# Rope in the head, gate columns turned, decays masked first: a change to a two-layer hybrid encoder on one Trainium2 core

## What is computed

```python
h = rms_norm(x, norm_mix_g)
u = h @ w_in                       # four mixers' columns
o_na = neighbourhood_attention(...)
h_fwd = mlstm_scan(qm, km, vm, gates[0], log_sigmoid(gates[1]))
h_bwd = flip(mlstm_scan(flip(qm), flip(km), flip(vm), flip(gates[2]), flip(log_sigmoid(gates[3]))))
o_ml = rms_norm(h_fwd + h_bwd, ml_norm_g) * sigmoid(qkvo[:, :, 3])
o_cv = conformer_conv(u_cv, ...)
qd = axial_rope(rms_norm(qd, att_q_norm_g)); kd = axial_rope(rms_norm(kd, att_k_norm_g))
o_at = blocked_gqa(qd, kd, vd)
proj = einsum('bsnc,ncd->bsnd', branches, w_branch)
g = sigmoid(h @ w_gate + b_gate)
x = x + (sum(g * proj) @ w_out)
x = x + hierarchical_moe(rms_norm(x, norm_ffn_g), ...)
```

## Time and profile before

| what | value |
|---|---|
| median of three runs | 2245.08 us (2244.16 to 2246.12) |
| the profiled execution's own time | 2239.99 us |
| its span | 2238.2 us |
| TensorE matmul busy | 91% of the span |
| VectorE, ScalarE, POOL busy | 43%, 23%, 15% |
| mean granted TensorE clock | 0.962 of full speed |

### The profile page before, as it was taken

One profiled execution on the slowest core, in us unless ns is written; L12 is line 12 of the kernel. 1 busy time (PEld: TensorE's weight loads), 2 busy tenths in 40 slices (PEclk: granted clock), 3 DMA queues, 4 the chain that ended last, 5 costly groups with the idle time before them and its releaser, 6 DMA issues. The chain is left out here.

```text
span 2238.2 us, 24086 instructions
## 1 busy us (share of the span) xinstructions
PE 2045.4 (91%) x8840; PEld 1274.6 (57%) x8840; DVE 965.6 (43%) x1820; ACT 524.9 (23%) x1114; POOL 339.3 (15%) x276
## 2 busy tenths in 40 slices
PE   7799999999999997999498999999999999969990
PEld 3455556555655554888245555645555655558870
DVE  1677615343545644111256773243444475431114
ACT  2133312344330001111122332124353100101111
POOL 1322220111110011000223122102211100110003
PEclk9999999999999998999799999999999999979995
DMA  5355557111116622998441121212110274159955
GB/s 203 151 198 210 232 196 299 54 66 66 66 57 249 239 92 106 368 365 308 177 182 38 66 80 52 76 38 97 73 66 26 108 284 195 57 230 343 371 203 178
DMA packets 67188, 361.85 MB, mean 162 GB/s; under 512 B 5760, under 2 KB 6144, under 8 KB 54016
## 3 DMA queue, kind: packets, MB, share of 16 engines
q1 hardware_dynamic: 42160, 276.40, 32.8%
q10 hardware_dynamic: 18000, 58.73, 6.5%
q0 software_dynamic: 6912, 25.17, 3.1%
HBM read 249.13 MB, written 111.15 MB: 161 GB/s over the span
## 5 line engine op out<-in xcount | busy, mean ns | idle before, releaser
L674 PE MATMUL bank<-x,ring 128*128 128x384 f32 x1056 | 374.6, 504 | 27.1 <-issue 27.1
L674 PE MATMUL bank<-hT,ring 128*128 128x384 f32 x1056 | 360.2, 490 | 3.2 <-issue 3.2
L674 PEld LDWEIGHTS bank<-x,ring 128*128 128x128 f32 x1056 | 199.7, 195 | 187.5 <-issue 73.8
L674 PEld LDWEIGHTS bank<-hT,ring 128*128 128x128 f32 x1056 | 195.9, 190 | 144.9 <-issue 21.4
L832 ACT ACTIVATE sums<-bank 128x384 f32<-128x384 f32 x132 | 64.9, 491 | 306.1 <-PE bank L674 304.4
L994 DVE SCALAR_TENSOR_TENSOR reg_a<-cvx,pp,reg_a 128x783 f32<-128x783 f32 x120 | 130.3, 1086 | 4.3
L659 PE MATMUL bank<-ring,hT 128*128 128x256 f32 (+1 forms) x384 | 125.4, 486 | 0.0
L972 DVE SCALAR_TENSOR_TENSOR gbuf<-bank,sums 128x384 f32<-128x384 f32 x96 | 53.5, 558 | 155.3 <-PE bank L674 108.4
L1719 DVE SCALAR_TENSOR_TENSOR prob<-prob,bank 128x256 f32<-128x256 f32 x30 | 12.6, 421 | 229.4 <-ACT prob L1539 229.4
L659 PEld LDWEIGHTS bank<-ring,hT 128*128 128x128 f32 x384 | 72.5, 190 | 49.1 <-issue 43.7
L506 PE MATMUL bank<-ring,hT 128*128 128x512 f32 x192 | 88.2, 614 | 5.3 <-ACT hT L525 5.3
(11 more groups left out here) (258 smaller groups left out, 2991.1 us busy)
## 6 DMA issues: line engine op xcount, KB each, us to landing
ring<-in_wd SPq DMA_DIRECT2D x29, 2048.0 KB, 9.8
blocks<-hT SPq DMA_DIRECT2D x16, 3072.0 KB, 21.3
gate_dram<-gbuf ACTq DMA_DIRECT2D x64, 384.0 KB, 2.3
ring<-gate_dram SPq DMA_DIRECT2D x16, 1536.0 KB, 6.4
oT<-in_we SPq DMA_DIRECT2D x8, 2048.0 KB, 11.4
ring<-in_we SPq DMA_DIRECT2D x8, 2048.0 KB, 11.9
wide<-in_we SPq DMA_DIRECT2D x8, 2048.0 KB, 11.1
reg_b<-in_we SPq DMA_DIRECT2D x8, 2048.0 KB, 11.4
```

The source lines that it names most:

```text
L674: mm = nc.tensor.matmul(bank[i % 2][:, 0:HALF], w[:, k, :], a[:, k, :], start=(k == 0 and r in (0, 1, 3)), stop=(k == 3), skip_group_check ...
```

## The change

1. Layer 0's first chunk of weights is loaded in two halves, with tile 1 between them, and the projection of a tile waits for the second half only at its fifth k-step. In both layers ScalarE evicts tile 0's transposes ahead of tile 1's squares. In layer 1 POOL's power of tile 0 stands ahead of one of the gathers.
2. Rope 0 leaves the list. VectorE does its piece 0 in the head ahead of tile 5's variance, and pieces 1 and 2 after tile 5's scaling; POOL's power of 18 columns stands ahead of tile 5's power. The halves of the gate bias move with it.
3. The 16 gate columns are appended to the output gate's 256 (`GATE_ROWS`). ScalarE copies them into `gate_cols`, tiles of 128 columns that POOL sets to zero once, and in place of each `mg` unit TensorE transposes three of these tiles. ScalarE's step `ctanh` comes after the fourth unit of `mo`, not the fifth.
4. The weighing is a step of its own, `weigh`. Where a decay follows the scores, its mask comes first on VectorE and the weighing behind it. For a short group both `dexp` steps stand ahead of the product, and three products instead of two follow each of its score steps that has a decay; in the long groups the third and fourth score steps are followed by one product instead of two. The number of products is the same.

```diff
-        if u == T // 2 - 1:
-            for piece in range(3):
-                add("rope", 0, piece)
...
-        if u == 4:
+        if u == 3:
             add("ctanh")
...
-    def decay(n, *key):
+    def decay(n, *key, weigh=None):
         add("decay", *key)
+        if weigh:
+            add("weigh", *weigh)
         add("dexp", *key, 0)
-        gate(n)
-        add("dexp", *key, 1)
+        if GROUPS[key[0]][1] == 2:
+            add("dexp", *key, 1)
+            gate(n)
+        else:
+            gate(n)
+            add("dexp", *key, 1)
...
             if q + 1 < len(pairs) and j < 2:
-                decay(1, *pairs[q + 1], j)
-                gate(1)
+                decay(1, *pairs[q + 1], j, weigh=(g, hp, j))
+                gate(2 if GROUPS[g][1] == 2 else 1)
             else:
-                gate(2)
+                add("weigh", g, hp, j)
+                gate(1 if j >= 2 else 2)
...
-                sp.dma_start(ring[:, 0, :], wd[0]).then_inc(head_in[0], 16)
-                for t in range(1, T):
+                sp.dma_start(ring[:, 0, 0:CW // 2], wd[0][:, 0:CW // 2]).then_inc(first_half, 16)
+                sp.dma_start(x[:, 1, :], tile_of(1)).then_inc(x_in[1], 16)
+                sp.dma_start(ring[:, 0, CW // 2:CW], wd[0][:, CW // 2:CW]).then_inc(head_in[0], 16)
+                for t in range(2, T):
...
-            if layer == 0:
-                head_square(act, layer, 1)
-                evict(0)
-            else:
-                evict(0)
-                head_square(act, layer, 1)
+            evict(0)
+            head_square(act, layer, 1)
...
+            rope(dve, done, 0, 0)
+            variance(T - 1)
+            scale(T - 1)
+            rope(dve, done, 0, 1)
+            rope(dve, done, 0, 2)
...
+                rope_power(pool, 0)
+                power(T - 1)
                 return
-            for t in (2, 3):
-                for c in range(TOP):
-                    gather(pool, t, c)
+            gather(pool, 2, 0)
+            gather(pool, 2, 1)
+            gather(pool, 3, 0)
             power(0)
+            gather(pool, 3, 1)
...
+            def gate_rows(i, name, u):
+                pe.wait_ge(proj_ev[i % 2], i // 2)
+                evicted(pe, at[("proj", "mo", T // 2 * (u + 1) - 1)])
+                for t in range(T // 2):
+                    mm = nc.tensor.transpose(bank[i % 2][:, t * P:(t + 1) * P], gate_cols[:, T // 2 * u + t, :], ident)
+                mm.then_inc(proj_mm, 1)
...
+                    done(activate(mlo[:, u, :], b[:, 0:BW], ACT.Tanh, scale=0.5))
+                    ins = activate(gate_cols[:, u, :].rearrange("p (q r) -> p q r", q=4)[:, :, 0:HEADS],
+                                   b[:, BW:BW + GATE_ROWS].rearrange("p (q r) -> p q r", q=4), ACT.Copy)
```

More of the change, by code:

```diff
@@ L35 @@
 BW = 256
+GATE_ROWS = 16
 HEADS = 4
@@ L497, in head_tensor @@
                     if k == 0:
-                        pe.wait_ge(head_in[0], 16 * (layer + 1))
+                        pe.wait_ge(first_half, 16) if layer == 0 else pe.wait_ge(head_in[0], 32)
                         pe.wait_ge(ht_ev, 2 * t + 1)
@@ L502, in head_tensor @@
                     if k == 4:
+                        pe.wait_ge(head_in[0], 16 * (layer + 1))
                         pe.wait_ge(ht_ev, 2 * t + 2)
@@ L544, in head_scalar, with evicted, rope @@
             project(T - 1)
+        def evicted(eng, i):
+            eng.wait_ge(proj_ev[i % 2], i // 2 + 1)
+            if i:
+                eng.wait_ge(proj_ev[(i - 1) % 2], (i - 1) // 2 + 1)
+        def rope(dve, done, part, piece):
+            h4 = lambda a: a.rearrange("p t (h d) -> p t h d", d=HD)
+            n = T // 2
+            tiles = slice(part * n, (part + 1) * n)
+            qk, tmp, cols = atr[:, tiles, 0:384], rope_tmp[:, tiles, :], slice(18 + 18 * part, 36 + 18 * part)
+            if piece == 0:
+                evicted(dve, at[("proj", "at", part * n + n - 1)])
+                done(tt(tmp, qk, qk, ALU.mult))
+                done(reduce_(msq[:, cols].rearrange("p (t h) -> p t h", t=n), h4(tmp), AX.X, ALU.add))
+                done(ts_(msq[:, cols], msq[:, cols], 1.0 / HD, EPS, ALU.mult, ALU.add), mix_var)
+            elif piece == 1:
+                dve.wait_ge(mix_rs, 1 + part)
+                r = rstd[:, cols].rearrange("p (t h) -> p t h", t=n).unsqueeze(3).to_broadcast([P, n, 6, HD])
+                done(tt(h4(qk), h4(qk), r, ALU.mult))
+                done(tt(qk, qk, rows[:, R_ATT:R_ATT + 384].unsqueeze(1).to_broadcast([P, n, 384]), ALU.mult))
+                for a in range(4):
+                    o, other = 16 * a, 16 * (a ^ 1)
+                    s = sin[:, tiles, o:o + 16].unsqueeze(2).to_broadcast([P, n, 6, 16])
+                    done(tt(h4(tmp)[:, :, :, o:o + 16], h4(qk)[:, :, :, other:other + 16], s, ALU.mult))
+            else:
+                done(tt(h4(qk), h4(qk), cos[:, tiles, :].unsqueeze(2).to_broadcast([P, n, 6, HD]), ALU.mult))
+                done(tt(qk, qk, tmp, ALU.add), rope_done)
         def head_vector(dve, layer):
@@ L604, in head_gpsimd @@
             gather(pool, 5, 1)
-            for t in range(2, T):
+            for t in range(2, T - 1):
                 power(t)
+            if layer < L:
+                rope_power(pool, 0)
+            power(T - 1)
         def load_chunk(sp, layer, c):
@@ L796, in mix_tensor @@
                     product(i, *key)
+                elif kind == "proj" and key[0] == "mg":
+                    gate_rows(i, *key)
                 elif kind in ("proj", "score", "ptrans", "attend", "turn", "decay", "mls", "ml"):
@@ L1207, in mix_gpsimd @@
                 if kind == "rope" and key[1] == 0:
-                    power(1 + key[0], 18 * key[0], 18)
+                    rope_power(pool, key[0])
                 elif kind == "cnorm":
@@ L1812, in laid_out @@
     for row, src in ((0, 0), (64, 4), (32, 8), (96, 12)):
-        last[:, :, BW + row:BW + row + 4] = w[:, :, gt + src:gt + src + 4]
+        last[:, :, BW + row // 8:BW + row // 8 + 4] = w[:, :, gt + src:gt + src + 4]
         pp[:, row:row + 4, PP_GB] = a["ml_gate_b"].reshape(L, 16)[:, src:src + 4]
```

90 lines of the change are left out of this document (38 added, 52 removed).

## The result

| | before | after |
|---|---|---|
| median of the runs, us | 2244.62 (4 runs, 2236.71 to 2246.12) | 2205.64 (4 runs, 2201.66 to 2208.06) |
| profiled execution, us (its span) | 2240.0 (2238.2) | 2208.1 (2206.2) |
| ratio | | 0.983, 95% interval 0.9813 to 0.9846 |

A forecast was written before the change was run, and what follows sets the result against it. TensorE, busy 2045 of 2238 us, was taken as the bound. Gains of 3.9 + 1.2 + 16.6 + 14.9 + 22.2 = 58.8 us off 2240.0 gave 2181.2, plus 5.1 for the median: 2186.3, range 2172 to 2204.

The forecast's parts named there:

- The failed step: In the mLSTM decays, after the change TensorE would have only small waits left, some 1.6 us in all.
- No instruction is added: In the mLSTM decays, the reordering was said to add no instruction to any engine.
- Head: Start of both layers: earlier first projection in layer 0, 3.9 us, and shorter POOL chain in layer 1, 1.2 us.
- the 1.2 of the forecast: Layer 1's start: one gather less before tile 0's power on POOL starts TensorE 1.2 us sooner.
- priced at a gain of 1.8: Layer 0's start: if the first half of the weights landed only at 15.3, the gain would be 1.8 us.
- Rope: Rotary work moved into the head: 9.72 us idle gone, waits of 0.8 and 2.3 us left; gain 16.6 us.
- one layer of two: The 2.3 us wait before product 6 lowers TensorE's clock in one of two layers, costing about 3.4 us.
- The rival without contention: Rotary work: POOL and VectorE don't collide and nothing waits; gain 26.2 us, time 2177; chance 0.17.
- Gates: mLSTM gates: 64 matmuls removed, 21.3 us, less added columns, transposes and waits; net gain 14.9 us.
- two of 0.5 and 0.6: mLSTM gates: TensorE waits of 0.5 and 0.6 us as cover goes, 2.2 us in both layers.
- Decays: mLSTM decays: TensorE's waits for ScalarE's exponentials and the low clock behind them mostly go; gain 11.1 us a layer, 22.2.
- ScalarE becomes the bound: mLSTM part: exponentials ahead of evictions and less cover give back half of 22.2 us; time 2197; chance 0.15.

The follow-up runs named there:

- experiment 1: Changed kernel with five instead of six products of fill in short groups and one instead of two in a long group's last step: 2181.27 us.
- experiment 2: Changed kernel, but SyncE issues the next weights' load only when the gates' stores have landed: 2177.86 us.
- before_with_late_load: Kernel before the change, with one edit alone: the load behind a gate chunk is issued after that chunk's stores have landed; 2229.45 us.
- no_gates_part: Changed kernel with the mLSTM gates computed as before, by 64 matmuls of 384 columns: 2218.74 us.

## Why the prediction was wrong

**The failed step** is in the decays, the sentence on what was left there: "0.5 at the first pair, 0.3 to 0.7 where the product with three ScalarE operations meets an exponential, some 1.6 in all". Those three waits came (0.51, 0.56 and 0.90 us), but two more came with them, 4.72 and 1.31 us, and behind the first the spell of lower clock, 4.5 us. So the part gained 1.7 us in the two layers and not 22.2. In its place the runs show (experiments 1 and 2): the fill moves products on VectorE's queue as well as on TensorE's. I had walked the fill as cover, product by product, against ScalarE's exponentials. I did not walk where its evictions fall on VectorE and what each of them waits for. "No instruction is added" was true and hid this. A moved step has to be asked the same as an added one: what is queued behind it, and which transfer it needs. The row was there to be read, in the waits of VectorE over the whole kernel before (us in total, times, longest):

```profile
DVE gbuf L972 <- DMA gate_dram<-gbuf: 39.1, 7, 7.7
```

The kernel after has 75.6 us in 9 there. Such a sum counts VectorE's whole idle time where the store came last, so it says where to look and not what it costs. Two of the seven stand in the mLSTM part (0.96 us at 578.44 and 1.46 in layer 1), ahead of nothing urgent, and held no scores up. The other five stand in the attention, and there TensorE already waited 7.7 us in all for the banks behind them and their like; `before_with_late_load` takes these waits away. In the changed kernel four stand in the mLSTM part, 7.3 to 11.3 us each, with the normalisation behind them.

**Head.** Forecast 5.1, undone 5.2. In layer 0 the first projection came at 11.88, not 13.2, as the scaling of tile 0 ended at 9.02 and not 10.48. By the other profiles that is no part of the edit: the first transposes begin at 9.61 to 10.63 in the three kernels without it and at 9.04 to 10.53 in the nine with it. From these transposes to product 0 the kernel takes 53.98 us before and 49.85 after, so the edit's share of the 5.6 is 4.1, for a forecast of 3.9. In layer 1 the wait ahead of the first transposes fell from 24.01 to 22.79 us, the 1.2 of the forecast, though the half clock near it took as much back. Both halves of the weights were there in time, the first by 11.88. The Trainium skill's page DMA: Bandwidth & Descriptors (Queues, rings and completion order) allows a landing out of order, which the prediction priced at a gain of 1.8; no run here shows one.

**Rope.** Right in each step, 18.2 for 16.6 (18.9 between the profiles). The wait of 2.24 us set off a spell of 3.41 us at 1.2 GHz in layer 0 and none in layer 1, as taken ("one layer of two"), by luck in part: in the profiles of the first two experiments the same wait of 2.24 us set off none in either layer. The rival without contention fell: 1.36 and 2.35 us for line 572 in one trace.

**Gates.** Forecast 14.9, undone 13.1, within the interval (13.8 between the profiles). 44.3 - 41.8 = 2.5 us for the 16 columns (forecast 2.6), 2.0 for the transposes (1.6), and one wait of 0.46 where I had walked two of 0.5 and 0.6.

**Decays.** Its mechanism was right, the waits for ScalarE fell from 13.0 to 1.0 us. Its size was right where the store isn't in the way (21.4 for 22.2; in experiment 1, 12.2 a layer for 11.1), and as built it came to nothing that the times can tell. The rival "ScalarE becomes the bound" gave a time nearer the measured one, 2197, for a reason that experiments 1 and 2 refute in the main: of its exponentials ahead of evictions 0.88 us of TensorE's 4.72 is left when the store is in time.

**Not forecast at all:** 2.7 us of longer waits in layer 0's first attention (5.6 for 2.9; layer 1's stayed at 2.9), again evictions behind late stores, gone in experiment 2. Why they grew is not settled. And the losses behind the branches' start, as said above.

## What to carry to other kernels

An instruction that waits long on an engine with time to spare is free only for what stands behind it in that engine's queue; before work is moved as fill, walk its evictions on their engine too, and list the waits, DMAs above all, that they carry along. A large load that nobody needs soon should be issued behind the small store that somebody does: here that order alone is worth 28 us of 2206, and 15 to 17 in the kernel before. And when an added gain fails to show, undo the parts one by one: three of four were worth what was forecast, which left one place to look first.

## What the runs showed that I had not expected

A store of 384 KB that was issued 2 us behind a load of 2 MB landed after 9.0 us, and after 2.6 with the load held back; the load took 10.5 and 8.7. So the small transfer pays most of the price, 6.4 us for 1.8: it lands when the large one does (554.1 and 553.6). The view of DMA queues between 535 and 565 us shows the load's queue with few, large packets and the store's with twice as many small ones (packets, MB, share of 16 engines):

```profile
q1 hardware_dynamic: 144, 2.10, 22.1%
q10 hardware_dynamic: 288, 0.79, 6.6%
```

That is 14.6 KB a packet against 2.7. The Trainium skill's page DMA: Bandwidth & Descriptors (Queues, rings and completion order) says that each DMA engine takes turns between queues by the packet and not by the byte. By that rule the store with twice the packets can't end before the load has sent its last, which is so here; but it should also have sent a packet for each of the load's from the time it was there. The trace doesn't agree with that. The same view from 546 to 548.8, 1 to 3.7 us behind the first store's issue (545.07), has no row for the store's queue at all, and the one from 548.8 to 551 has both:

```profile
q1 hardware_dynamic: 65, 1.06, 102.2%
```

```profile
q1 hardware_dynamic: 30, 0.39, 70.2%
q10 hardware_dynamic: 42, 0.13, 14.4%
```

With the load held back the store's queue moves 58 packets within 1.3 us of the issue. So beside the load the store sends nothing for 3.7 us, which turns by the packet don't explain, and takes part only when 100 of the load's 144 packets have gone (35 of them before 546). What holds it until then is open, and a test with other packet sizes was not made.

Two pairs of VectorE's multiplies with two inputs in SBUF and POOL's operations look like turns by whole instructions. At 45.81 VectorE's came 0.02 us first and took its 1.36 us, and POOL's took 2.47; at 68.93 POOL's came first and took 1.27, and VectorE's took 2.35, nearly the 1.13 that were left of POOL's and its own 1.36. The Trainium skill's GPSIMD Engine Reference (Key points) names the contention without a size; here it is 1.0 to 1.2 us on the instruction that comes second.

A wait of 2.24 us in front of the same product (the one at 78.31 after the change) was followed by 3.41 us at 1.2 GHz in layer 0 of two profiles (the changed kernel's and `no_gates_part`) and by none in the other five that have the wait, nor in layer 1 of any, in the same place with the same work before it. For single waits of this length a chance is the most that can be forecast, as the prediction did.
